# Two transformer blocks on one core: the first loads in half pieces over two queues, warm-up on the ones matrix, and the first quarter of x turned ahead of the gain

## What is computed

```
def first_block(x, norm_mix_g, w_in, ...):
    h = rmsnorm(x, norm_mix_g[layer])     # x: (1, 512, 1024)
    proj = h @ w_in[layer]                # w_in: (1024, 5888), used in slabs of 128 columns
    ...
def reference(...):
    x = first_block(x, norm_mix_g, ...)
    return second_block(x, meta_tokens_2, ...)
```

## Time and profile before

| | |
|---|---|
| runs, median of 3 | 1405.52 us (1405.17 to 1405.78) |
| the profiled execution, own time | 1404.8 us |
| its span (first to last instruction) | 1403.1 us |
| TensorE busy | 1395.6 us, 99% of the span |
| VectorE, ScalarE, GpSimd busy | 921.5, 596.1, 211.8 us |
| mean DMA rate over the span | 115 GB/s |
| records of matmuls | 8746 |

### The profile page before, as it was taken

The page is one execution under the profiler, slowest core; times in us unless marked ns, Lnnn a source line. Parts: engine busy times, 40 slices in busy tenths (PEclk is TensorE's granted clock), DMA queues, the critical chain, the costliest instruction groups (busy, mean ns, idle before and its releaser), DMA issues.

```text
span 1403.1 us, 21789 instructions
## 1 busy us (share of the span) xinstructions
PE 1395.6 (99%) x8746; PEld 1186.4 (85%) x8746; DVE 921.5 (66%) x1248; ACT 596.1 (42%) x842; POOL 211.8 (15%) x215
## 2 busy tenths in 40 slices
PE   9999999999999999999999999999999999999998
PEld 7898879777888989989888997778888998989886
DVE  6635433765767858587656778556756967758775
ACT  4324532554434435253244435344434535344353
POOL 4000000000022402111333020000022221303310
PEclk9999999999999999999999999999999999999999
DMA  5224123211336846635232322232225774927573
GB/s 184 90 91 113 61 71 101 70 46 45 120 101 155 196 119 152 165 101 150 97 103 86 91 69 76 72 98 86 90 90 140 182 162 114 212 90 195 134 176 109
DMA packets 154860, 161.61 MB, mean 115 GB/s; under 512 B 4010, under 2 KB 144660, under 8 KB 154788
## 3 DMA queue, kind: packets, MB, share of 16 engines
q1 hardware_dynamic: 122868, 129.12, 29.1%
q0 software_dynamic: 31904, 31.46, 12.4%
q10 hardware_dynamic: 16, 0.00, 0.0%
HBM read 157.68 MB, written 2.10 MB: 114 GB/s over the span
## 4 chain that ended last, share of the span: by engine, by line
PE 99%; ACT 0%; DVE 0%; issue 0%; POOL 0%; POOLq 0%; ACTq 0%
PE ps L2355 63%; PE ps L2420 17%; PE ps L2351 4%; PE ps L2377 4%; PE ps L2493 3%; PE ps L2748 1%; PE ps L2563 1%; PE ps L2777 1%; PE ps L2867 1%; PE ps L2763 1%; PE ps L2652 0%; PE ps L2695 0%; PE ps L2949 0%; PE ps L2713 0%; PE ps L2659 0%; PE ps L2479 0%
## 5 line engine op out<-in xcount | busy, mean ns | idle before, releaser
L2355 PE MATMUL ps<-AA,wh 128*128 128x512 f32 x1440 | 453.7, 396 | 0.0
L2355 PE MATMUL ps<-BB,wh 128*128 128x512 f32 x1088 | 342.2, 396 | 0.2 <-issue 0.2
L2355 PEld LDWEIGHTS ps<-AA,wh 128*128 128x128 f32 x1440 | 267.4, 188 | 62.7 <-DVE wl L1449 0.8
L2355 PE MATMUL ps<-AA,wl 128*128 128x512 f32 x720 | 283.4, 394 | 0.0
L915 ACT ACTIVATE wh<-raw 128x1024 fp32r<-128x1024 f32 (+2 forms) x149 | 141.5, 950 | 260.3 <-PE ps L2355 206.5
L2355 PEld LDWEIGHTS ps<-BB,wh 128*128 128x128 f32 x1088 | 202.2, 188 | 49.6 <-issue 1.8
L2355 PE MATMUL ps<-BB,wl 128*128 128x512 f32 x544 | 213.9, 393 | 0.0
L1449 DVE TENSOR_TENSOR wl<-raw,wh 128x1024 fp32r<-128x1024 f32 (+2 forms) x149 | 169.9, 1140 | 60.6 <-ACT wh L915 60.3
L2355 PEld LDWEIGHTS ps<-AA,wl 128*128 128x128 f32 x720 | 135.4, 188 | 31.0
L2355 PEld LDWEIGHTS ps<-BB,wl 128*128 128x128 f32 x544 | 102.3, 188 | 23.3
L2420 PE MATMUL ps<-Hl,wh 128*128 128x256 f32 x384 | 108.2, 282 | 0.0
(11 more groups left out here) (408 smaller groups left out, 2411.5 us busy)
## 6 DMA issues: line engine op xcount, KB each, us to landing
raw<-in_w_in SPq DMA_DIRECT2D x38, 1024.0 KB, 5.4
raw<-in_w_ff SPq DMA_DIRECT2D x31, 1024.0 KB, 5.4
raw<-in_w_mlp_in SPq DMA_DIRECT2D x16, 1024.0 KB, 5.4
raw<-in_w_mlp_out SPq DMA_DIRECT2D x16, 1024.0 KB, 5.2
zf<-in_w_mlp_out POOLq DMA_DIRECT2D x48, 256.0 KB, 4.5
zf<-in_w_ff POOLq DMA_DIRECT2D x48, 256.0 KB, 4.6
raw<-in_w_out SPq DMA_DIRECT2D x8, 1024.0 KB, 5.2
arena<-in_x SPq DMA_DIRECT2D x4, 512.0 KB, 6.7
```

Source lines behind the costliest of these rows:

```text
L2355: last = pe.matmul(dense_psum(t_ps, kind), a[:, k, :], b[:, o0 + k, col0:col0 + S1], start=start, stop=stop)
```

## The change

The diff does five things.

1. x's first quarter is loaded as two pieces of 128 columns (256 KB each; the first signals `x_early`), and x1 follows at once on SP's queue.
2. The first quarter of the weights is loaded as two pieces of one block each (128 KB; the first signals `w_early`), and these and w1 are issued by ACT, behind the gain and ahead of its table load. SP issues only w2 and w3.
3. POOL writes the ones matrix first. TensorE warms up on it, with 5 matmuls, as soon as it is written, and then turns block 0 of x before the gain.
4. The high parts (POOL) and low parts (DVE, `first_low`) of blocks 0 and 1 of the weights are made piece by piece; the waits on `w_first_hi` and `w_first_lo` count accordingly.
5. TensorE's order has lh(1) ahead of turn_x(2).

```
+        def first_load(k, n):
+            return (raw[:, 0, k * 256:(k + n) * 256].rearrange("p (k n) -> p k n", k=n),
+                    weight_view("w_in", 0, KT, 2 * P)[:, k:k + n, :])
...
-            for q in range(4):
-                load_x(q)
-                sp.dma_start(raw[:, 0, q * S1:(q + 1) * S1].rearrange("p (k n) -> p k n", k=2),
-                             weight_view("w_in", 0, KT, 2 * P)[:, 2 * q:2 * q + 2, :]).then_inc(w_first[q], 16)
+            load_x(slice(0, P), x_early)
+            load_x(slice(P, 2 * P), x_in[0])
+            load_x(slice(256, 512), x_in[1])
+            for q in range(2, 4):
+                load_x(slice(q * 256, (q + 1) * 256), x_in[q])
+                sp.dma_start(*first_load(2 * q, 2)).then_inc(w_first[q], 16)
...
+            pool.memset(ones[:, :].bitcast(F32), 1.0).then_inc(consts_ready, 1)
             after(pool.memset(ident[:, :], 0.0))
-            pool.memset(ones[:, :].bitcast(F32), 1.0).then_inc(consts_ready, 1)
...
-            convert_first(0, w_first_hi)
+            for k, landed in enumerate((w_early, w_first[0])):
+                pool.wait_ge(landed, 16)
+                pool.tensor_copy(first_weights(wh, 0)[:, :, k], first_raw(0)[:, :, k]).then_inc(w_first_hi, 1)
...
             act.dma_start(grow[0:KT, :], d["norm_mix_g"][0].rearrange("(a b) -> a b", b=P)).then_inc(gain_in, 16)
+            act.dma_start(*first_load(0, 1)).then_inc(w_early, 16)
+            act.dma_start(*first_load(1, 1)).then_inc(w_first[0], 16)
+            act.dma_start(*first_load(2, 2)).then_inc(w_first[1], 16)
...
+            def first_low(k):
+                dve.wait_ge(w_first_hi, k + 1)
+                dve.tensor_tensor(first_weights(wl, 0)[:, :, k], first_raw(0)[:, :, k], first_weights(wh, 0)[:, :, k],
+                                  ALU.subtract).then_inc(w_first_lo, 1)
+
             x_lo(0)
-            convert_first(0, w_first_hi, 1, w_first_lo)
+            first_low(0)
             x_lo(1)
+            first_low(1)
             convert_first(1, hi_ready, 1, lo_ready)
...
-                pe.wait_ge(x_in[m // 2], 16)
+                pe.wait_ge(x_early if m == 0 else x_in[m // 2], 16)
...
-                    pe.matmul(ps[:, 1, 0:P], ident[:, :], ident[:, :], start=True, stop=True)
-
+                    pe.matmul(ps[:, 1, 0:P], ones[:, :].bitcast(F32), ones[:, :].bitcast(F32), start=True, stop=True)
+
+            pe.wait_ge(consts_ready, 1)
+            warm(5)
             pe.wait_ge(consts_ready, 2)
-            warm(6)
+            turn_x(0)
             pe.wait_ge(gain_in, 16)
...
-            turn_x(0)
             turn_x(1)
             first_hh(0)
             first_hh(1)
             first_lh(0)
             first_hl(0)
+            first_lh(1)
             turn_x(2)
             turn_x(3)
-            first_lh(1)
             first_hl(1)
```

More of the change, by code:

```diff
@@ L312, in build @@
         w_first = [sem(f"w_first{i}") for i in range(3)] + [w_landed[0]]
+        x_early, w_early = sem("x_early"), sem("w_early")
         w_first_hi, w_first_lo = sem("w_first_hi"), sem("w_first_lo")
@@ L624, in _, with load_x @@
         def _(sp):
-            def load_x(i):
-                at = slice(i * 256, (i + 1) * 256)
+            def load_x(at, landed):
                 sp.dma_start(xnat[:, :, at], d["x"][0].rearrange("(a p) d -> p a d", p=P)[:, :, at])\
-                  .then_inc(x_in[i], 16)
+                  .then_inc(landed, 16)
             def params():
@@ L1872, in _ @@
             x_lo(3)
-            convert_first(2, w_first_hi, 2, w_first_lo)
+            convert_first(2, w_first_hi, 3, w_first_lo)
             x_lo(4)
@@ L2566, in first_hh @@
                 if k % 4 < 2:
-                    pe.wait_ge(w_first_hi, 1 + k // 4)
+                    pe.wait_ge(w_first_hi, 1 + k if k < 4 else 3)
                 else:
@@ L2580, in first_hl @@
                 if k % 4 < 2:
-                    pe.wait_ge(w_first_lo, 1 + k // 4)
+                    pe.wait_ge(w_first_lo, 1 + k if k < 4 else 3)
                 else:
@@ L2605, in _ @@
             turn_x(7)
-            pe.wait_ge(w_first_lo, 2)
+            pe.wait_ge(w_first_lo, 3)
             for t in range(2):
```

## The result

| | before | changed |
|---|---|---|
| median | 1405.51 us (22 runs, 1404.59 to 1406.54) | 1408.23 us (22 runs, 1405.76 to 1409.48) |
| profiled execution, own time | 1404.8 | 1408.01 |
| its span | 1403.1 | 1406.3 |

The changed kernel is slower: ratio 1.0019, 95% interval 1.0013 to 1.0025, so 2.7 us. That is just inside the 0.2% that I called "no change", and outside my range of 1404.3 to 1406.3. The runs of the changed kernel also scatter over 3.7 us, those of the old one over 2.0.

A forecast was written before the change was run, and what follows sets the result against it. TensorE, busy 1395.6 of 1403.1 us, bounds the kernel, so only the start could change. A gain of 0.45 gave 1404.8 - 0.45 = 1404.35 profiled and 1405.5 - 0.45 = 1405.1 us median, range 1404.3 to 1406.3.

The forecast's parts named there:

- no change: Whole kernel: the forecast move was under the 0.2% (2.8 us) that a measurement can tell, so it counted as none.
- my range of 1404.3 to 1406.3: Whole kernel: forecast bounds on the median around 1405.1 us; a clock staying low lay outside.
- the sum: Whole kernel: 0.45 us gained at the start, taken off 1404.8 for a profiled execution and 1405.5 for the median.
- Ones first: TensorE's start: warm-up begins at 1.07 instead of 1.66 and ends at 3.6 instead of 4.59.
- The landings of x: First loads: x0's first half lands at 3.9, its second at 5.3; first product at 5.85 instead of 6.46.
- The second weight piece: First stretch: no landing of its own forecast; from the second pair on, products follow at 2 x 0.235 each.
- the two queues only share: Rival, 20%: at the first loads, ACT's pieces delay x's second half to 5.8; gain 0.05, time 1405.5.
- the rival that I gave 12%: First stretch: breaks in TensorE's work put off the rise to 2.4 GHz; 1.6 us slower, 1407.1; chance 12%.
- 0.3 of ACT's wait as hidden: First stretch at the low clock: 0.3 of the 2.35 us extra for ten products disappears in an existing wait, leaving 2.05.
- Slab 2: Next late point after the start: DVE's chain must move earlier too; it has 0.55 of slack, so the gain holds.
- the cap: DVE's chain, stopped by w3's cast, limits the gain to 0.55 us.
- Within 0.2%: Whole kernel: measured time differs from before by less than 2.8 us either way; given 0.96.

The follow-up runs named there:

- e6: Kernel before, old whole-quarter loads, with ones matrix first, eight warm-up matmuls on it and block 0 turned ahead of the gain: 1405.24 against 1405.25 us.
- e2: Changed kernel plus seven filler matmuls, results never read, between hh(0) and hh(1): 1407.53 us against 1405.01 for the kernel before.
- e3: Changed kernel with lh(0) and hl(0) moved ahead of hh(1): 1405.93 us against 1405.01 for the kernel before.
- e5: Changed kernel with seven instead of five warm-up matmuls: 1406.67 us against 1405.25 for the kernel before.
- e8: Changed kernel with seven warm-up matmuls, one more ahead of turn_x(1), and lh(0), hl(0) ahead of hh(1): 1405.86 us against 1405.25 for the kernel before.
- e4: Kernel before, old loads, with ones matrix first, five warm-up matmuls on it and block 0 turned ahead of the gain: 1406.64 against 1405.01 us.
- e7: Kernel before with three instead of six warm-up matmuls, nothing else changed: 1406.28 against 1405.25 us.
- e9: Changed kernel with loads on SP's queue alone, seven warm-up matmuls, one more ahead of turn_x(1), lh(0), hl(0) ahead of hh(1): 1405.83 us against 1405.16 before.
- e12: Kernel before with ones matrix first, six warm-up matmuls on it, and x0 loaded in two halves on SP's queue: 1406.67 against 1405.12 us.
- e1: Changed kernel with all first loads, still in half pieces, issued by SP on one queue: 1407.20 us against 1405.01 for the kernel before.
- e11: Run e1 with seven instead of five warm-up matmuls: 1405.87 us against 1405.16 for the kernel before.
- e10: Run e6 with w0 and w1, whole, issued by ACT behind the gain instead of by SP: 1406.07 us against 1405.16 for the kernel before.

## Why the prediction was wrong

Two steps of it failed: the wait for the second weight piece, which the sum left out, and the clock, which the sum took as high. In detail:

- **Ones first: right, and worth nothing.** TensorE started at 1.07 as worked out, and the warm-up ended near 3.57. e6 shows that the earlier start buys nothing as long as x lands when it does.
- **The landings of x: right.** First transpose 3.90 (I had 3.9), second half at 5.3 (5.3), first high part at 5.30 (5.1), first product at 6.13 (5.85). ACT's three issues took 0.37, 0.50 and 0.52 and its table load ran from 2.96 to 4.24, covered as worked out. But these landings are no better than the old ones where it counts: the old kernel had both blocks of x0 at 4.4. I compared the first half with the whole and did not ask what the second half costs.
- **The second weight piece: the sum's first failed step.** I wrote that "hh(1), lh(0), hl(0), lh(1) follow at 2 x 0.235 each" and gave w0b no landing of its own, taking both pieces as there with w0's old 5.3. It landed at 7.9 (in the profiles of e2, e3, e5 and e8, with the same loads, its cast starts at 6.8 to 7.7) and cost 1.68 between hh(0) and hh(1). The rival "the two queues only share" had the right place, but it made x late, not the weights, and its price was 0.4 us.
- **The clock: the rival that I gave 12%.** It was priced at 1407.1, and its mechanism is what e4, e6 and e7 show: a break of 0.9 to 1.0 us between the warm-up and the first transposes puts off the rise from near 5 to near 9, even where it delays no instruction. I argued against it that the breaks are 0.3 to 0.5 each. e2's profile has 0.52 and 0.15 and the low clock; the profile after has 0.33 and 0.33 and the high one until 6.8, then loses it in the wait of 1.54. So breaks as short as these make it a matter of the run, and the forecast rested on the good draw. Its price was worked out with 0.3 of ACT's wait as hidden; the earlier trace rows have 0.17, since eight products with 1.88 of work fill the 2.05 from 6.46 to 8.51.
- **What the rival left out.** It tied the late rise to breaks alone. e9 and e12 had it (at 10 and 12.6) after unbroken work from 1.07 to 5.2 and longer, so something else that differs from run to run has a part in it; these runs do not show what. The last microsecond of that work is transposes, and no run tests whether they keep the clock up as products do.
- **The point that I missed about the old warm-up.** The earlier trace rows show TensorE working from 1.66 to 5.9 with nothing longer than a tenth between. I read the six warm-up matmuls as cover until x0 lands. They are that, but their end at 4.59, just past the landing at 4.4, is also what keeps the work unbroken. The change starts them 0.6 earlier and takes one away, so they end a microsecond sooner, 0.3 before their data.
- **Slab 2: not reached.** I had capped the gain by DVE's chain. The chain moved with TensorE, 3.0 later at slab 2, and the cap never came into play.
- **The verdict.** "Within 0.2%" holds by a hair at 1.0019; the range and the sign of the expected move do not.

The sizes can be set side by side, each against its own runs of the kernel before, by medians and, in brackets, by the ratios: two queues and short warm-up 2.7 us (2.7); one queue and short warm-up 2.2 (1.8, e1); two queues and longer warm-up 1.4 (2.0, e5); one queue and longer warm-up 0.7 (1.4, e11). By medians the warm-up is the larger part; by ratios the queue is, and the four intervals overlap. So the runs show that both cost time (e4 and e5), and not how the 2.7 us divide. The longer warm-up with the old loads is back at zero (e6). What remains of the half pieces with a longer warm-up is 0.6 to 0.7 by medians (e8, e9, e11), which single intervals do not separate from zero except for e11; the later landings of the second pieces are in each of their profiles.

The second queue's weights land late because that queue gets the smaller share of the traffic (e10); why it does is not settled by these runs. The Trainium skill ("DMA: Bandwidth & Descriptors", section "Issuing engines are not separate DMA queues") says that only issue time is saved, and the times agree that nothing was won. The Trainium skill (the same page, section "Queues, rings and completion order") has each engine take turns between its queues, a packet at a time; by that ACT's queue would have half of the traffic as long as both have work and their packets are alike. e10's trace shows that from 4.5 to 5.5 (0.18 and 0.19 MB), and less for ACT's queue, 0.18 against 0.34 MB, from 5.5 to 7.0. The changed kernel's trace does not show half: from 3.0 to 7.0 SP's queue moved 0.17, 0.18, 0.22 and 0.26 MB in the four microseconds and ACT's 0.10, 0.04, 0.08 and 0.06, a quarter of the whole, while ACT still had over 0.2 MB to move.

## What to carry to other kernels

A warm-up is measured by where it ends, not by where it starts: it must reach past the landing of the first data on a bad day, since a matmul too many costs 0.43 us at most (two records 0.21 apart) and a break of 0.9 to 1.0 ahead of the first work cost 1.0 to 1.6 us here, though nothing waited for what stood in it. It is no guarantee (e9, e12), so a start has to be judged by many runs, and one profile may show the rarer case. When a first load is cut in pieces, work out when the last piece lands that the third or fourth instruction needs; the first piece alone buys nothing if the engine then stops behind it. And work that needs data already present belongs ahead of the work that waits for the next piece.

## What the runs showed of the hardware that I had not expected

- The level of the clock after a broken warm-up differs between executions of one program: the same start had 128-column transposes 0.11 us apart at 5.4 in one profile and 0.21 apart in another, and the times of e11 fall in two groups 2 us apart. The Trainium skill ("TensorE: Matmul & The Clock Gate", section "Part 1: The HAM clock gate (the "warmup" mystery)") says that the number of slow matmuls at the start varies from run to run of one kernel; the traces agree.
- The granted clock of the profile read 1.00 while TensorE ran at half speed at the start, in every kernel; it read 0.50 only after a fall from the high level.
- A load of w0 issued 0.2 us later, from another engine and with nothing ahead of it on its own queue but 4 KB, landed 1.4 us later (e10): its bytes began to move at 4.0, when x0's were through, and then shared the engines with SP's next loads.
- With x0 in two halves of 512-byte rows, w0, which kept its 1 KB rows and had the same bytes ahead of it, landed 1.5 us later in the one profile taken, 0.6 of it by its later issue (e12).
- With 512-byte rows the full engines moved 265 GB/s, with 1 KB rows 363 (e12 and the kernel before, 3.0 to 4.0).
